# Two operand splits moved behind the evacuation at nine tiles of each layer, and one weight load moved ahead of eight small ones, in a two-layer decoder trunk

## The reference

```
h = rmsnorm(x, norm_g[i])
proj = h @ w_in[i]           # its columns are split among all that follows
ya = forgetting_attention(qa, ka, va, logf) * silu(za)        # 8 heads x 64
kcmp = (silu(blocks(kcb) @ cmp_w1_k + b1)) @ cmp_w2_k          # compressed keys; values alike
yb = nsa_attention(qb, ...compressed, selected, window...) * silu(zb)
yc = differential_attention(qc, kc, vc) * silu(zc)
merged = sum_j sigmoid(mg_j) * (y_j @ w_br_j)                  # j = a, b, c
x = x + merged @ w_out
x = x + sigmoid(x @ w_ple_gate) * (p[i] @ w_ple)
```

## Time and profile before

| | us |
|---|---|
| median of three runs | 1498.74 (1497.97 to 1499.55) |
| the profiled execution | 1496.63 |
| its span, first to last instruction | 1494.8 |
| PE busy | 1469.7 |
| DVE busy | 946.6 |
| ACT busy | 628.0 |

### The profile page before, as it was taken

One profiled execution on the slowest core, in us unless ns is written; L12 is line 12 of the kernel. 1 busy time (PEld: TensorE's weight loads), 2 busy tenths in 40 slices (PEclk: granted clock), 3 DMA queues, 4 the chain that ended last, 5 costly groups with the idle time before them and its releaser, 6 DMA issues.

```text
span 1494.8 us, 21863 instructions
## 1 busy us (share of the span) xinstructions
PE 1469.7 (98%) x7765; PEld 1227.9 (82%) x7765; DVE 946.6 (63%) x2197; ACT 628.0 (42%) x1499; POOL 74.7 (5%) x79
## 2 busy tenths in 40 slices
PE   8999999999999999999999999999999999999997
PEld 6788888888888888888877887888888888878885
DVE  6866766655556676465677667656555667754544
ACT  6543434434344444243444334344344444434333
POOL 1000000000001000000100000000000000000011
PEclk9999999999999999999999999999999999999998
DMA  6334453234235543432342345422343355433322
GB/s 166 94 86 120 106 121 79 64 84 101 77 77 135 140 114 92 115 104 71 99 111 72 105 113 132 102 64 71 87 97 78 102 128 133 118 106 92 103 75 92
DMA packets 259264, 150.51 MB, mean 101 GB/s; under 512 B 47482, under 2 KB 247764, under 8 KB 259156
## 3 DMA queue, kind: packets, MB, share of 16 engines
q1 hardware_dynamic: 259156, 149.11, 38.4%
HBM read 118.67 MB, written 2.10 MB: 81 GB/s over the span
## 4 chain that ended last, share of the span: by engine, by line
PE 89%; DVE 4%; ACT 2%; issue 2%; DMA 1%; SPq 1%; POOL 0%; ACTq 0%; POOLq 0%; DVEq 0%
PE D L764 23%; PE D L766 22%; PE D L765 22%; PE Ob L955 7%; PE T L933 4%; PE S L921 2%; PE S L920 2%; PE S L910 1%; DVE w_lo L1310 1%; PE Mb L971 1%; PE Mb L845 1%; PE Ob L959 1%; DMA arena<-rcs 1%; ACT w_hi L1081 1%; PE D L777 1%
## 5 line engine op out<-in xcount | busy, mean ns | idle before, releaser
L764 PE MATMUL D<-h_hi,w_hi 128*128 128x512 f32 x1264 | 537.5, 425 | 2.7 <-DVE zs L1459 2.7
L766 PE MATMUL D<-h_lo,w_hi 128*128 128x512 f32 x1264 | 496.0, 392 | 0.0
L765 PE MATMUL D<-h_hi,w_lo 128*128 128x512 f32 x1264 | 494.3, 391 | 0.0
L1310 DVE TENSOR_TENSOR w_lo<-raw,w_hi 128x512 fp32r<-128x512 f32 (+2 forms) x504 | 292.4, 622 | 162.5 <-ACT w_hi L1081 162.2
L1189 ACT ACTIVATE probs<-probs,nmax 128x128 f32<-128x128 f32 (+3 forms) x256 | 142.0, 556 | 399.1 <-DVE nmax L1559 399.1
L1081 ACT ACTIVATE w_hi<-raw 128x512 fp32r<-128x512 f32 (+2 forms) x504 | 256.7, 558 | 60.7 <-DMA raw<-in_w_in_dram 44.9
L766 PEld LDWEIGHTS D<-h_lo,w_hi 128*128 128x128 f32 x1264 | 237.2, 188 | 53.1
L764 PEld LDWEIGHTS D<-h_hi,w_hi 128*128 128x128 f32 x1264 | 238.8, 189 | 43.7 <-issue 4.6
L765 PEld LDWEIGHTS D<-h_hi,w_lo 128*128 128x128 f32 x1264 | 239.4, 189 | 30.4 <-issue 0.5
L1559 DVE CUSTOM_DVE_ANT_0 probs<-S,maskb 128x128 f32<-128x128 f32 (+3 forms) x256 | 115.2, 487 | 40.9 <-PE S L921 25.0
L546 DVE COPY pT<-T 128x128 f32<-128x128 f32 (+3 forms) x160 | 77.7, 488 | 80.4 <-PE T L933 80.0
(11 more groups left out here) (249 smaller groups left out, 1607.0 us busy)
## 6 DMA issues: line engine op xcount, KB each, us to landing
raw<-in_w_in_dram SPq DMA_DIRECT2D x124, 512.0 KB, 4.0
arena<-rcs SPq DMA_DIRECT2D x48, 256.0 KB, 4.4
raw<-in_w_in_dram SPq DMA_DIRECT2D x32, 256.0 KB, 4.0
arena<-rcs SPq DMA_DIRECT2D x64, 128.0 KB, 2.3
raw<-in_w_out_dram SPq DMA_DIRECT2D x16, 512.0 KB, 3.6
raw<-in_w_ple_gate_dram SPq DMA_DIRECT2D x16, 512.0 KB, 3.6
rcs<-rx SPq DMA_DIRECT2D x80, 64.0 KB, 2.0
raw<-in_cmp_w_k_dram SPq DMA_DIRECT2D x8, 512.0 KB, 3.8
```

Source lines behind the costliest of these rows:

```text
L764: pe.matmul(o, w_hi[:, sl, cs], hi[:, k, :], start=(k == 0), stop=False)
L765: pe.matmul(o, w_lo[:, sl, cs], hi[:, k, :], start=False, stop=False)
L766: ins = pe.matmul(o, w_hi[:, sl, cs], lo[:, k, :], start=False, stop=last)
L1310: TT(w_lo[:, sl, half], raw[:, ring(L, t, RAW), half], f(w_hi[:, sl, half]), ALU.subtract).then_inc(M["dve_lo"], 1)
```

## The change

The function `evacuates_first` picks tile 0 and every tile with a quarter tile behind it. For those, ACT and DVE take `hi(t + 2)` and `lo(t + 2)` after their evacuation instead of before it. And in layer 1 SP issues the load of tile 2 ahead of its wait for `dve_x` and of the eight small loads.

```diff
+def evacuates_first(tiles, t):
+
+    return t == 0 or t + 1 < len(tiles) and tiles[t + 1][0] in ("w1k", "w1v")
...
                     if L:
+                        static_load(RAW)
                         sp.wait_ge(MM[L - 1]["dve_x"], NM)
...
-                    for t in range(RAW, 4):
+                    for t in range(RAW + (L > 0), 4):
                         static_load(t)
...
                             D = Dn[ring(L, t, 2)]
-                            hi(t + 2)
+                            if not evacuates_first(tiles, t):
+                                hi(t + 2)
                             if kind in ACT_EVAC:
                                 act.wait_ge(M["pe_dense"], t + 1)
...
                             if kind in ("w1k", "w1v") and n == 3:
                                 act.wait_ge(M["dve_evac"], dve_evac.after(t))
                                 A(hth, hacc, ACT.Tanh, scale=0.5).then_inc(M["act_hid"], 1)
+                            if evacuates_first(tiles, t):
+                                hi(t + 2)
...
                             Db = Dn[ring(L, t, 2)]
-                            lo(t + 2)
+                            if not evacuates_first(tiles, t):
+                                lo(t + 2)
                             if kind in DVE_EVAC:
                                 dve.wait_ge(M["pe_dense"], t + 1)
...
                                     TT(acc[:, n, :], acc[:, n, :], rt[:], ALU.add).then_inc(M["dve_acc"], 1)
+                            if evacuates_first(tiles, t):
+                                lo(t + 2)
```

## The result

| | before | changed |
|---|---|---|
| median, 22 runs each | 1497.99 us | 1500.23 us |
| ratio, 95% interval | | 1.0015 (1.0008 to 1.0021) |
| profiled execution: span | 1494.8 us | 1499.0 us |

The changed kernel is 2.2 us slower, 1.2 to 3.1 by the interval: 0.15%. The forecast was +2.1 us. One disturbed run of the changed kernel is left out of the ratio.

The account below looks back on a forecast made before the run. PE, busy 98% of the span, was taken to bound the kernel, so only its pauses count. Quarter-tile places +4.26 us less 2.14 us at first tiles gave +2.1 us, 1500.8 us; range 1495.6 to 1504.4 us.

Parts of the forecast that it names:

- The floor: Quarter-tile places: from ScalarE's evacuation start to PE's start at tile t+2 takes 1.99 us, 2.14 where VectorE evacuates too.
- Tile 12's 0.04: At tile 12, 2.14 us needed against 2.10 us of cover, so 0.04 us lost per layer.
- The backlog at tile 15: Two low halves delay VectorE's row maxima by 1.20 us, so PE waits for the exponential; 0.88 us per layer in all.
- The rival of more such places: VectorE's delay reaches PE through the softmax at three more places per layer: 3.6 us more, 1504.4 us; chance 20%.
- Tile 31: `th` and `zs` are evacuated earlier, PE starts at 196.86, not 197.41: 0.55 us won; a low half is then last.
- Layer 1's first tile: Evacuating `va` 0 first, or moving tile 2's load, each alone wins PE's 1.44 us pause there.
- Layer 0's first tile: Evacuating first at tile 0 wins 0.70 us of PE's pause, with bounds 0 and 0.87.
- The faster rival: The bank binds and low halves stay out of PE's way everywhere: 3.24 us gained, 1495.5 us; chance 15%.
- Late loads: Loads of t+4 go out 1.2 to 3 us later, priced at nothing; as a rival 1504.8 us at most, chance 7%.
- The signs: Right: `zs`, `va` 0 waits go, `w_lo` waits at 25, 27, 29. Wrong: tile 27 under 1.5 us after evacuation, `raw` waits.
- The sum: Whole kernel: +4.26 - 2.14 = +2.1 us, giving 1500.8 us against the median; chance 58%, own range 1498.5 to 1503.0.
- The forecast's two summands of opposite sign: Quarter-tile places cost +4.26 us over two layers; the first tiles of both layers gain 2.14 us together.

Follow-up runs that it names:

- quarter_only: Against the kernel before: new order only at the eight tiles with a quarter tile behind them, tile 0 and the load as before; 1501.18 against 1497.51 us, ratio 1.0027.
- place_25: Against the kernel before: new order at tile 25 alone; tile 27 starts 0.78 us later in both layers.
- dve_order_only: Against the kernel before: at the eight quarter-tile places only VectorE evacuates first, ScalarE keeps high halves first; span 1501.9 us.
- dummy_13: Kernel before with two unused VectorE additions, about 1.2 us together, behind VectorE's evacuation of tile 13; tile 15 on time, tile 16 0.94 us late.
- two_places_load27: New order only at tiles 0 and 29, moved load, and tile 27's load ahead of four swap transfers; 1494.23 against 1497.30 us for the kernel before, ratio 0.9981.
- first_only: Against the kernel before: new order at tile 0 alone, load of tile 2 where it was; 1495.38 us, ratio 0.9985.
- two_places: Against the kernel before: new order only at tiles 0 and 29, with the moved load; 1494.98 us, ratio 0.9982.
- dummy_29: Kernel before with two unused VectorE additions, 1.2 us together, ahead of `zs` of tile 29; tile 31 starts 1.21 us later, takes 1.60 longer (2.84 in layer 1).

## Why the prediction was right, point by point

- **The floor** (evacuation to weights ready, in a row) was right in kind at tiles 25, 27 and 29: `quarter_only`, `place_25` and `dve_order_only` take it apart. Its size was 1.99 us and it measured 1.90. The term that was off is PE's start after VectorE's end: I took 0.15 us from the earlier trace rows, where it is behind `zs`; behind a low half it is 0.05 to 0.06 (179.68 to 179.74). So the starts of tiles 25, 27 and 29 came out 0.1 less late (0.25, 0.78, 0.46 for 0.34, 0.87, 0.55) and the gain at tile 31 0.1 higher (0.65 for 0.55). Tile 12's 0.04 vanished by the same error. Tile 25 loses 0.09 more inside itself: its second matmul follows the first, which now stands behind a short pause, at 0.34 us (170.35 to 170.69), where it followed at 0.23. Nothing in the forecast had this, so that the total there (0.34) equals the forecast is luck.
- **The backlog at tile 15**: 0.93 us measured, 0.88 forecast. `dummy_13` shows its cause. The rival of more such places fell: in the first four attention stages PE has no other new wait for an exponential, and tiles 17 and 20 start on time.
- **Tile 31**: the bank was indeed last there, and the low half took its place.
- **Layer 1's first tile**: 1.49 us in the traces against the first profile of before, 1.44 forecast; that either edit alone wins it was right. But the old pause varies with the load's landing, which came 4.40 to 5.21 us after its issue (4.93 in the profile that the forecast was read from). Against the eight profiles with the old order and the old load the changed kernel wins 0.95 to 1.77 us here, 1.25 on average. The forecast read one execution, whose pause was longer than that of all but one of the others.
- **Layer 0's first tile**: 0.70 forecast, 0.39 and 0.31 in the two profiles of the changed kernel. It goes with the clock. Seven of the fourteen profiles, among them the second of before and both of the changed kernel, have a stretch of half clock between 11.3 and 16.1 us. With it tile 1 starts 0.2 to 1.0 us late. The old order at tile 0 hides most or all of that in the pause behind it: from tile 0's start to tile 2's, its profiles with the stretch agree with the first profile of before, which has none, within 0.13 us. The new order has no such pause to hide it in, and wins 0.39, 0.31 and 0.62 (`two_places_load27`) with the stretch, 0.83 and 0.84 (`first_only`, `two_places`) without it. That the stretch makes the difference is read from these profiles; no run sets it.
- **The faster rival** (the bank binds) held at one place of eight, tile 31. The Trainium skill's Perfetto Trace Analysis, section Optimizing Tensor Performance, has matmul groups rotate through PSUM banks so that an evacuation overlaps the next group's matmuls. Freeing the bank first everywhere, as the prediction read it, would have made `quarter_only` faster, and that is the part that is slower, by 4.0 us.
- **Late loads** cost nothing, as priced, but they didn't stay away. While tile 31 runs, ScalarE now waits 0.60 us (layer 0) and 1.15 us (layer 1) for the load of tile 33, and before that 0.19 and 0.40 us for that of tile 14; the profiles of before have neither wait. By its words on tiles 16 to 31 the prediction would have taken the first two as a sign that it was wrong. They move no tile start: tile 33's step is 0.00 in both layers.
- **The signs.** Both old waits are gone, as forecast. Tile 27 starts 1.90 us after `y_f`'s evacuation, above the 1.5 that was to mean wrong. PE waits for a low half at 27 and 29, but only 0.21 us at 29, and at 25 no wait shows, though the tile starts late. From tile 10's start to tile 31's the layers became 1.82 and 1.89 us longer, for 2.1.
- **The sum.** From the marks, tile 0 to tile 32 of each layer, first profile: -0.39 + 1.85 - 1.49 + 1.96 = +1.9 us; second: -0.31 + 1.90 - 1.49 + 1.95 = +2.0. The runs say +2.2 (1.2 to 3.1). The other 2.2 us by which the first profile was longer (4.1 in all; 4.2 by the rounded spans) are elsewhere: tile 0 began 0.60 us later, the stretches behind tile 32 of layer 0 lost 0.6, and 0.9 lie behind the last dense matmul. That these are scatter of executions and not the change is shown by size, not place by place: the unaltered kernel has up to 1.9 us of it.

The forecast's two summands of opposite sign were measured apart: +4.0 us (2.4 to 5.7; forecast +4.3) for the quarter-tile places, and -2.2 (-0.9 to -3.4; forecast -2.1) for the first tiles. These intervals are too wide to test the terms; the marks are finer. By them the places cost 3.8 us and the first tiles of the changed kernel gave 1.8 to 1.9 against the first profile of before, about 1.6 if layer 1's 1.25 is taken (3.8 - 1.6 is the +2.2 of the runs). So both summands were forecast 0.3 to 0.5 us too large, and that the net came out at the forecast is in part luck.

## What to carry to other kernels

Where work A and work B stand in one in-order queue and both feed the same consumer, putting A first helps only where A was the later of the two. Compare for each place the cover (from the trigger to the consumer's start) with the sum of what now runs in a row; a rule by tile kind, as here, took the one good place of the eight together with four that cost and three that change nothing. And count what is queued behind the moved work: at tile 15 nine tenths of the cost came through a softmax that has nothing to do with the tile.

## What the runs showed of the hardware

- A pause of PE can cost more than its own length. Behind pauses of 1.73 us (`dve_order_only`) and 2.56 us (`dummy_29`) the granted clock fell from 2.4 to 1.2 GHz in both layers, and tile 31 took 1.6 us longer (2.8 in layer 1 of `dummy_29`). Behind the 1.35 us pause of the kernel before it stayed at full. I had priced pauses one for one. The Trainium skill's TensorE: Matmul & The Clock Gate, section "Part 1: The HAM clock gate (the "warmup" mystery)", says that the gate watches how busy PE is and passes either all or half of the clock's pulses; these traces agree with the two levels.
- ScalarE and VectorE overlap neighbours that aren't held by a wait: high halves of 0.62 us follow at 0.52, low halves of 0.69 at 0.60. The floor came out right only with these distances.
- One load of 512 KB, tile 27's in layer 1, took 4.1 us to land in the first profile of before and 5.3 to 5.8 in four others, issued at the same point of the schedule. ScalarE then waited 0.37 to 0.89 us for it, and the tile started later by 0.27 us less than that, 0.10 to 0.62. The other tile starts from 12 to 32 repeat to 0.06 us where the order is the same.
